# Two attentions of a fused two-block transformer: units worked in pairs, value products in two column groups, step functions on two engines

## What is computed

```python
# selected attention ("dsa"): 128 keys per query, chosen by an index score
s = einsum('bqhd,bqkd->bqhk', q_b, k_sel) * attn_scale
s = s + moveaxis(rel_bias[t5_bucket(pos_sel - qpos)], -1, 2)
p = softmax(where(valid, s, -inf));  o = einsum('bqhk,bqkd->bqhd', p, v_sel)
# latent attention ("mla")
s = (einsum('bqhd,bshd->bhqs', qn, k_nope) + einsum('bqhr,bsr->bhqs', qp, k_pe)) * scale
p = softmax(where(key < (q // 64 + 1) * 64, s, -inf));  o = einsum('bhqs,bshd->bqhd', p, v)
```

## Time and profile before

| | us |
|---|---|
| runs shown | 2269.19, 2276.17, 3470.2 |
| median of the runs | 2276.17 |
| profiled execution | 2269.23 |
| its span | 2267.4 |
| latent attention | 1521.9 to about 1589.5 |
| selected attention | 1656.4 to about 1752.0 |

### The profile page before, as it was taken

One profiled execution on the slowest core, in us unless ns is written; L12 is line 12 of the kernel. 1 busy time (PEld: TensorE's weight loads), 2 busy tenths in 40 slices (PEclk: granted clock), 3 DMA queues, 4 the chain that ended last, 5 costly groups with the idle time before them and its releaser, 6 DMA issues.

```text
span 2267.4 us, 26064 instructions
## 1 busy us (share of the span) xinstructions
PE 2103.3 (93%) x10158; PEld 1669.1 (74%) x10162; DVE 961.8 (42%) x1547; ACT 801.9 (35%) x1159; POOL 707.2 (31%) x298
## 2 busy tenths in 40 slices
PE   6899998779899999999999999789989998999998
PEld 3788766567788878778887877655855877888887
DVE  2614584962433440143344334665677313223101
ACT  3431245322443421344432133535234324434212
POOL 0322100122344444334444423220310433444442
PEclk8999999868899999999999999999979999999999
DMA  7533200000343353324335522210210222232221
GB/s 313 197 129 112 75 1 20 19 1 19 117 156 144 139 186 102 102 92 157 141 139 195 187 78 84 65 47 1 75 38 1 84 85 73 93 102 93 95 95 60
DMA packets 59839, 221.52 MB, mean 98 GB/s; under 512 B 6768, under 2 KB 7024, under 8 KB 58224
## 3 DMA queue, kind: packets, MB, share of 16 engines
q1 hardware_dynamic: 59472, 220.13, 27.7%
q10 hardware_dynamic: 288, 0.33, 0.0%
HBM read 218.33 MB, written 2.10 MB: 97 GB/s over the span
## 4 chain that ended last, share of the span: by engine, by line
PE 55%; issue 21%; DVE 10%; POOL 9%; ACT 4%; DMA 1%; SPq 0%; POOLq 0%; DVEq 0%; ACTq 0%
PE ps L375 44%; POOL w_lo L1453 9%; ACT prob L914 1%; PE ps L1983 1%; DMA raw<-stream 1%; PE ps L506 1%; PE ps L1852 1%; PE ps L1832 1%; PE ps L1061 1%; DVE prob L960 1%; PE ps L1973 1%; PE ps L1963 1%; DVE t L565 1%; PE ps L1958 1%; DVE neg_max L947 1%
## 5 line engine op out<-in xcount | busy, mean ns | idle before, releaser
L1453 POOL TENSOR_TENSOR w_lo<-raw,w_hi 128x1024 fp32r<-128x1024 f32 x284 | 686.6, 2418 | 1450.8 <-ACT w_hi L387 804.1
L375 PE MATMUL ps<-hh,w_hi 128*128 128x512 f32 (+1 forms) x1576 | 629.3, 399 | 37.7 <-POOL w_lo L1453 19.6
L375 PE MATMUL ps<-hl,w_hi 128*128 128x512 f32 (+1 forms) x1576 | 622.9, 395 | 0.0
L375 PE MATMUL ps<-hh,w_lo 128*128 128x512 f32 (+1 forms) x1576 | 622.5, 395 | 0.0
L375 PEld LDWEIGHTS ps<-hh,w_hi 128*128 128x128 f32 (+1 forms) x1576 | 301.2, 191 | 111.6 <-POOL w_lo L1453 21.6
L375 PEld LDWEIGHTS ps<-hh,w_lo 128*128 128x128 f32 (+1 forms) x1576 | 300.8, 191 | 65.3
L375 PEld LDWEIGHTS ps<-hl,w_hi 128*128 128x128 f32 (+1 forms) x1576 | 301.2, 191 | 62.4
L1434 ACT ACTIVATE w_hi<-raw 128x1024 fp32r<-128x1024 f32 x132 | 140.1, 1061 | 298.7 <-PE ps L375 298.3
L1479 DVE TENSOR_TENSOR prod<-silu,ps 128x512 f32<-128x512 f32 x66 | 45.4, 688 | 414.5 <-PE ps L375 392.1
L375 PE MATMUL ps<-act_hi,w_hi 128*128 (+1 forms) x528 | 209.3, 396 | 8.1 <-POOL w_lo L1453 8.1
L375 PE MATMUL ps<-act_lo,w_hi 128*128 (+1 forms) x528 | 209.1, 396 | 0.0
(11 more groups left out here) (387 smaller groups left out, 2424.7 us busy)
## 6 DMA issues: line engine op xcount, KB each, us to landing
raw<-stream SPq DMA_DIRECT2D x316, 512.0 KB, 3.6
mod_raw<-late SPq DMA_DIRECT2D x72, 512.0 KB, 4.0
mod_w<-mod_w SPq DMA_DIRECT2D x8, 1024.0 KB, 15.9
xT<-xT SPq DMA_DIRECT2D x2, 1024.0 KB, 16.0
out<-fin SPq DMA_DIRECT2D x8, 256.0 KB, 2.0
csta<-csta SPq DMA_DIRECT2D x1, 1344.0 KB, 20.4
cT<-cT SPq DMA_DIRECT2D x1, 1024.0 KB, 20.3
cond<-cond SPq DMA_DIRECT2D x1, 512.0 KB, 24.1
```

The lines of the kernel that those rows point to most:

```text
L375: mm = pe.matmul(out, w, r, start=first and i == 0, stop=last and i == 2)
L1453: pool.tensor_tensor(w_lo[g % SPLIT][:, :], raw[n % RING][:, :], w_hi[g % SPLIT][:, :].bitcast(F32), ALU.subtract)\
```

## The change

Units become pairs of units. In the latent attention a pair is two heads of one query block, in the selected one two neighbouring units. Scores of a pair go to two neighbouring banks (0 and 1, or 6 and 7), so that one memset, one maximum and one reciprocal serve both; exponentials, scalings, transposes and copies stay one per unit (z = 0, 1). `mp` and `mpT` hold pairs. The value products of z = 0 and z = 1 alternate, block by block, and write rows 0 to 63 and 64 to 127 of one bank. In the selected attention the bank is copied out after four pairs in four instructions on each engine. TensorE's order in a round changes from scores, turn, values to turn, scores, values. The steps of z = 1 are done by GpSimd (`dsa_gpsimd`), into a ring of 16 tiles.

```diff
-    mp = [sb(f"mp{i}", [P, N]) for i in range(2)]
-    mpT = [sb(f"mpT{i}", [P, NT, P]) for i in range(2)]
+    mp = [sb(f"mp{i}", [P, 2, N]) for i in range(2)]
+    top[0] = region_ki
+    mpT = [sb("mpT0", [P, 2, NT, P])]
+    top[0] = region_sq
+    mpT.append(sb("mpT1", [P, 2, NT, P]))
-    NSTEP = 8
+    NSTEP = 16
...
-    score_banks = (0, 1, 6)
-    mla_units = [(h, qt) for h in range(H2) for qt in range(NT)]
+    pair_banks = (0, 6)
+    mla_pairs = [(hp, qt) for hp in range(H2 // 2) for qt in range(NT)]
...
+        def mix_values(p):
+            for z in range(2):
+                read(pe, ("mt", p, z))
...
             for t in range(qt + 1):
-                mm = pe.matmul(ps[rows, ob, qt * P:(qt + 1) * P], vbt[:, t, h * DH2:(h + 1) * DH2], mpT[u % 2][:, t, :],
-                               start=(t == 0), stop=(t == qt))
+                for z in range(2):
+                    h = 2 * hp + z
+                    mm = pe.matmul(ps[64 * z:64 * z + 64, ob, qt * P:(qt + 1) * P], vbt[:, t, h * DH2:(h + 1) * DH2], mpT[p % 2][:, z, t, :],
+                                   start=(t == 0), stop=(t == qt))
...
-        for u in range(len(mla_units)):
-            if u + 2 < len(mla_units):
-                scores(u + 2)
-            turn(u)
-            if u:
-                mix_values(u - 1)
+        for p in range(len(mla_pairs)):
+            turn(p)
+            if p + 2 < len(mla_pairs):
+                scores(p + 2)
+            if p:
+                mix_values(p - 1)
...
+        def maxima(p):
+            hp, qt = mla_pairs[p]
+            keys, b = (qt + 1) * P, pair_banks[p % 2]
+            for z in range(2):
+                full(dve, ("ms", p, z))
+            mark("mla_step", dve.memset(ps[0:64, b:b + 2, keys - 64:keys], NEG))
             settle(dve, "mla_step")
+            dve.tensor_reduce(sm["mla_max"][p % 2][:, :], ps[:, b:b + 2, 0:keys], AX, ALU.max, negate=True).then_inc(S("mla_max"), 1)
...
+            for z in range(2):
+                read(dve, ("ms", p, z))
+            mark("mla_step", dve.reciprocal(sm["mla_inv"][p % 2][:, :], sm["mla_sum"][p % 2][:, :]))
             settle(dve, "mla_step")
+            for z in range(2):
+                dve.tensor_scalar(mp[p % 2][:, z, 0:keys], mp[p % 2][:, z, 0:keys], sm["mla_inv"][p % 2][:, z:z + 1], None, ALU.mult)\
+                   .then_inc(S("mp_ready"), 1)
+            if p + 2 < len(mla_pairs):
+                maxima(p + 2)
+            if p:
+                outputs(p - 1)
...
+    def steps(e, p, z, done):
+        if p >= 2:
+            full(e, ("ds", p - 2, z))
+        for j in range(4):
+            i = 8 * p + 4 * z + j
+            e.tensor_scalar(step_of(p, z, j)[:, 0:pair_keys(p)], posf[:, 0:pair_keys(p)], qfrom[:, i:i + 1], None, ALU.is_ge)\
+             .then_inc(S(done), 1)
+
+    def dsa_gpsimd(pool):
+        read(pool, ("pb", KD - 1))
+        for p in dsa_pairs:
+            steps(pool, p, 1, "step_ready_pool")
...
-        split_lows(pool, ffns["ffn2"]["g1"] + KF, ffns["ffn3"]["g0"])
+        split_lows(pool, ffns["ffn2"]["g1"] + KF, second["g_gated_a"] + 2)
+        dsa_gpsimd(pool)
+        split_lows(pool, second["g_gated_a"] + 2, ffns["ffn3"]["g0"])
```

## The result

The changed kernel takes 2278.8 us (median of nine runs) against 2270.2 for the kernel before on the same chips, a ratio of 1.0035 with a 95% interval of 1.0020 to 1.0049; one of the nine runs of the kernel before, 3470.2 us, was slow and doesn't enter the ratio. The profiled execution has a span of 2275.4 us, 8.0 above before's 2267.4. That is within the 2% that count as no change, on the slow side, and half of the 16 us forecast.

The account below looks back on a forecast made before the run. TensorE, busy for 93% of the span, bounds the kernel before; the new order's ring of waits then sets both attentions' pace. Latent +4.6 and selected +11.5 make 16.1 us on 2269.2: 2285, range 2250 to 2312.

Parts of the forecast that it names:

- The ring: Both attentions: scaling, transposes, scores two pairs on, maxima, next scaling wait in a circle; 4.1 us a pair in the latent.
- the formula: Ring length for n blocks, n' two pairs later: latent 1.4+0.70n'+0.24n us, selected 1.43+0.91n'+0.24n, at full clock.
- Value products halved: Each attention: alternating column groups cut TensorE's value products from 19.6 us to about 10.9.
- The clock in the latent attention: Latent attention: 40% of the time at the lower clock makes 62.3 us 69.3, ending 4.6 later than before.
- GpSimd's collisions: Selected attention: scalings wait behind GpSimd's steps, 1.4 us a ring at n=4, 10 us in all.
- GpSimd's step: Selected attention: one step on GpSimd takes 0.1+0.2n us, 0.9 at 512 columns, with ends 0.45 and 1.3.
- The clock, +14: Selected attention: half of the time at the lower clock adds 14 us.
- Start-up: Selected attention: start-up takes 7.2 us, GpSimd's first steps standing behind w_lo, first scaling at about 1664.9.
- The clock holds: Rival, both attentions: granted clock stays at 0.92 or more; 2264 us, or 2256 with fast steps; chance 0.25.
- GpSimd is slow: Rival, selected attention: 1.3 us a step, 11 us more, 2296, or 2312 with the clock low; chance 0.2.
- That the ring does not bind: Rival, both attentions: TensorE stays the bound, -19 and -22 us, 2228; chance 0.07.
- that the column groups do not overlap: Rival, value products: they save no TensorE time, only the copy-outs grow, 2288 us; chance 0.05.

Follow-up runs that it names:

- Experiment 1: The changed kernel with scores of pair p+2 issued ahead of the transposes of pair p in both attentions: 2234.4 us, ratio 0.9855 to the kernel before.
- experiment 4: The changed kernel with the value products of both attentions issued twice: 2277.2 us, ratio 1.0032 to the kernel before.
- experiment 5: The kernel before with only the transposes of unit u moved ahead of the scores of unit u+2, both attentions: 2315.1 us, ratio 1.0204 to the kernel before.
- experiment 2: The changed kernel with scores of pair p+2 ahead of transposes of pair p and all steps on VectorE: 2227.0 us, ratio 0.9815 to the kernel before.
- experiment 3: The changed kernel with all steps of the selected attention on VectorE, new order kept: 2275.2 us, ratio 1.0030 to the kernel before.
- experiment 7: As experiment 2, but value products of head 0 ahead of the next pair's transposes, those of head 1 behind: 2234.5 us, ratio 0.9857 to the kernel before.

## Why the prediction was right, and where its sizes were off

**The ring: right.** The forecast took the order to close a ring that leaves TensorE's saved work idle. Experiment 1 opens it and gets 28 us back in the latent attention; experiment 4 doubles the saved work for 0.2 us over both stages; experiment 5 puts the same ring into the kernel before and loses 25 us. Its rings held within 0.35 us in all four kinds of round at full clock, each a little too long (the formula itself gives 2.8 for the 2.9 of the third). The transposes waited for the scalings in 15 of 16 pairs, as said, for 1.3 us on average instead of 0.7 to 1.1.

**Value products halved: right.** 25.5 us became 15.0. Of the 4.1 over the forecast's 10.9 the low clock explains 2.7, for experiment 2 has 12.3 at 0.96. The other 1.4 were the forecast's: it took ten times a row of 16 records, and the shorter rows are dearer per record (4, 8, 12 and 16 take 0.44, 0.66, 0.88 and 1.09 us there).

**The clock in the latent attention: right in sign, a little small.** The forecast had 40% of the time at the lower level and +4.6 us; the stage's granted clock was 0.75, half of the time at 1.2 GHz, and the stage 6.8 longer. With half instead of 40% the forecast's own sum gives 71.4 us instead of 69.3, and +6.8. That it comes out so exactly is in part luck, since its rings were 0.1 to 0.35 us too long each.

**The selected attention: mis-sized.** +11.5 us was the forecast, +0.8 came. The largest error is the term for GpSimd's collisions: 10 us in the sum, between 1 and 4 by the rings and the scalings.

- *GpSimd's step.* I took 0.9 us at 512 columns with 1.3 as the slow end; it is 1.73 on average. Its own rows by size (0.62, 0.96, 1.31, 1.73) are near 0.25+0.37n. I had put it halfway between the fill and the two-tensor operation, while per column (3.4 ns) it is above both. The Trainium skill (GPSIMD Engine Reference, "Engine selection") calls one-input operations roughly line-rate; the measurement decides against that here, for this operation with fp32 in and bf16 out.
- *The collisions, 10 us.* I had both scalings of a ring stand behind a whole step, 0.8 to 1.4 us each. They did not: the longest of the 32 took 0.84, and two of 384 columns at 1731.68, with GpSimd's steps beside them, took 0.75 together, as the two at 1553.93 in the latent attention with GpSimd idle. The means by size are 414, 506, 599 and 527 ns against 284, 351, 418 and 483 without GpSimd (experiment 3), for 32 scalings 4.1 us in all. The 527 hides that six of its eight scalings come after GpSimd's last step, which ends at 1744.97, and take 484; the two before take 0.49 and 0.83. The Trainium skill (SBUF — State Buffer, "Who interferes with whom") has one of the two engines blocked for the length of the other's instruction when VectorE's is in a two-port mode; no row names the mode, and beside these steps nothing was held for that long. Beside the w_lo it was the earlier trace rows. Which property of GpSimd's instruction makes the difference is open. VectorE's steps were slowed as well, from 0.48 to 0.74. Experiment 3 prices the whole use of GpSimd there at 3.8 us, net of the four more steps a pair that VectorE then has.
- *The clock, +14.* The stage's granted clock was 0.81, so 38% of the time at the lower level and not half; by the same formula (29 us over all rings) that is 11.
- *Start-up.* The first transposes come 10.4 us after the first keys, because TensorE waits for GpSimd's steps, which start only at 1665.72 behind the w_lo; the forecast had the first scaling some 8.2 after them, which makes about 2 us too little.

The rings themselves tell collisions from clock. Four of the changed kernel, from transposes to transposes, with (n, n') = (1, 2), (1, 2), (3, 3) and (3, 4), columns as in the earlier trace rows:

```profile
1679.60:1684.50 4.90, 4.10 (x36) 2.55 (x36) 3.02 (x9) 1.32 (x7) 4.26 (x6) 0.61 0.00 0
1684.50:1688.10 3.60, 2.52 (x37) 1.67 (x37) 3.15 (x9) 1.57 (x9) 3.60 (x4) 1.00 0.02 5
1718.60:1726.10 7.50, 6.46 (x48) 4.00 (x48) 4.77 (x9) 1.79 (x5) 4.53 (x4) 0.62 0.01 2
1726.10:1732.20 6.10, 4.75 (x48) 2.61 (x49) 4.89 (x9) 2.00 (x6) 6.10 (x4) 1.00 0.00 0
```

Eight of the fourteen rings have TensorE's records at the full level. Without their copy-outs they add up to 39.9 us, and the forecast's formula without collisions gives 39.0, though GpSimd works in all eight. So the collisions show as about 1 us there. The formula ran 0.1 to 0.35 us a ring too long in the latent attention; if it does so here, they are some 2 to 4 us, near the 4.1 by which the scalings grew, and in no reading 10. The other six, at granted clocks of 0.50 to 0.72, take 33.3 us instead of 23.3; the formula for the lower level gives 9.6 of these 10. The account then reads 85.1 (the forecast's 84.1, from the start used here), 1.8 for the start-up, 0.9 and 10 in the rings, and 0.8 for a longer tail, within 0.2 us of the 98.5 measured; the forecast had 10 and 14 where 0.9 and 10 stand.

The two rounds from four blocks to four bear this out. The timeline of TensorE in the changed kernel has their transposes at

```profile
1737.83 1.40 PE L1996 MATMUL ps<-cst,mp 128*128 128x128 f32 x8 [1.19 <-DVE mp L2132]
...
1747.12 1.97 PE L1996 MATMUL ps<-cst,mp 128*128 128x128 f32 x8 [4.29 <-DVE mp L2132]
...
1755.10 1.09 PE L1996 MATMUL ps<-cst,mp 128*128 128x128 f32 x8 [0.97 <-DVE mp L2132]
```

The first is 9.3 us with the copy-outs in it, 6.1 without their 3.2, near the formula's 6.0. The second is 8.0 with neither a copy-out nor a step of GpSimd in it, at a granted clock of 0.72. "Every 7 us or so" is thus their mean and fits neither, and what lengthened the second was the clock and not the collisions that I gave.

**The rivals.** "The clock holds" did not happen (0.75 and 0.81, the bar was 0.92). "GpSimd is slow" happened as a fact but not as a price: at 1.73 us it ought to have cost more than the 11 us I gave it, and did not, because its collisions are mild and TensorE waited for its steps only once. Only once the ring is gone do they bind (experiments 1 and 2, 9.6 us). That the ring does not bind, and that the column groups do not overlap, are ruled out (experiments 4 and 7).

**The sum.** +6.8 and +0.8 in the stages, 0 between them, -1.8 ahead and +2.1 behind, together 8.0. The last two lie outside what was changed, and are scatter from one execution to the next: over the thirteen traces of this document, which run the same work there, the latent attention begins between 1515.5 and 1526.8 us, and the stretch behind the selected one takes 511.4 to 515.2. The forecast of 2285 against 2278.8 lies in its range because the latent attention came as said, and in spite of 10.7 us too many in the selected one.

**What the change would have been worth.** Its pairs and column groups are good and its order and GpSimd's steps are not. With the order undone and the steps back (experiment 2) the kernel is 1.9% faster than before: 21.1 us less in the latent attention and 22.6 in the selected one. Of the 21.1, 7.3 come from the column groups (experiment 7). The other 13.8 come with the pairs: from the kernel before to experiment 7 waits for the scalings fell from 7.6 to 0.3 us, and the clock rose from 0.93 to 0.97. Which of the two brought how much was not separated, nor was pairing tried apart from its larger banks of scores.

## What to carry to other kernels

Before pricing the work that a change removes, write down each engine's queue order and follow who waits for whom from one round to the next. Work that an engine does between its own producer and consumer in that ring is time, all else is cover. A cheap test of which it is: double it and look whether the stage grows, with the granted clock beside it, for the added work can raise that. When two loops are merged into one, keep the scores of the later round ahead of the instruction that waits for the slow engine; a swap of two calls was worth 28 us in one stage here and 14 in the other, more than all else in the change.

## What the runs showed of the hardware that I had not expected

- A GpSimd comparison with a per-partition scalar, fp32 to bf16, takes 0.62 us at 128 columns and 1.73 at 512; VectorE alone does the same in 0.34 and 0.48. GpSimd's 1.73 is a mean of 1.56 with neither a step nor a scaling of VectorE beside it (one starts at 1743.41) and up to 1.98. Half of the steps on GpSimd took only 4 us off VectorE's busy time (71.3 to 67.2), since both engines slow each other.
- The two column groups of TensorE overlap without alternating, as long as few records stand before the group changes: 8 records head by head 0.66 us, as alternating; 12 in 1.15 instead of 0.88; 16 in 1.58 instead of 1.09. When other matmuls stand between, 4+4 take 0.65 each and 8+8 take 1.09 each.
- More work can shorten a stage. With the value products doubled the granted clock of the latent attention rose from 0.75 to 0.91, and the stage went from 75.5 to 73.2 us.
